# Expert slots through a table in memory, the residual kept on the chip, logits from uncentred rows

## The chip, the cores and the metric

One core of a Trainium2 chip runs the whole program. The time is device microseconds (us) of one execution. Its engines run side by side, each its own list of instructions in the order in which it was written, and wait for one another on semaphores: TensorE (PE), VectorE (DVE), ScalarE (ACT), GpSimd (POOL) and SyncE (SP). DMAs are issued by SP, ACT and POOL and carried out by 16 DMA engines.

## The reference

A two-layer trunk over 512 tokens of width 1024, all in fp32. Layer 0 mixes with chunked gated linear attention (GLA), layer 1 with forgetting attention (FoX); after each mixer comes a layer norm and a mixture of 16 experts:

```python
h = layer_norm(ALPHA * h + mix, ln_g[layer, 0], ln_b[layer, 0])
ffn = grouped_moe(h, router_w, router_bias, moe_w_gate[layer], moe_w_up[layer], moe_w_down[layer])
h = layer_norm(ALPHA * h + ffn, ln_g[layer, 1], ln_b[layer, 1])

def layer_norm(x, g, b):
    mu = mean(x); var = mean((x - mu) ** 2)
    return (x - mu) * rsqrt(var + 1e-5) * g + b

def grouped_moe(x, router_w, ...):            # x: 512 x 1024
    scores = softmax(x @ router_w)            # 16 experts in 4 groups
    # best group by the sum of its top-2 scores (+ bias), then the top-2 experts inside it
    gates = ...                               # two nonzero weights a token, summing to 1
    h = silu(x @ w_gate[e]) * (x @ w_up[e])   # for each expert e, width 512
    y = sum over e of (gates[:, e] * h) @ w_down[e]
```

## The kernel before

There are T = 4 tiles of 128 rows, K = 8 slices of 128 columns and E = 16 experts. An fp32 product is made as three faster ones, of the high and low parts of both sides (L717, L718, L719). A weight comes from memory into a ring in SBUF, ACT casts it to its high part, DVE subtracts that to get the low part, PE uses both.

**Weights.** SP loads them in the order of use: pieces of 2 MB for the mixers (L458), halves of 1 MB for the experts (L506). A load into a ring slot that was used before waits on `w_free`, which PE raises by a marker, a tiny product (L758) at the end of the last unit that reads the slot. A unit is one row tile by 512 columns, 24 products. Between pieces SP issues small loads: the router weights and the layer norms' `ln_b` (L475, L477) behind the piece n == 3.

**GLA.** The units are followed by the heads. For each head and tile PE makes an output in one of two PSUM banks (L1099, L1104), ACT copies it out (L1513) and squares it (L1517); PE reuses a bank when ACT has copied it.

**Entry of the experts.** The out-projection's units add to the residual `H` (DVE, L1649, L1652). DVE subtracts the mean and multiplies by `ln_g` (L1661), then multiplies by the inverse deviation and adds `ln_b` (L1694). PE turns the centred rows (`turn_centred`, L814), ACT copies them, PE makes the router's logits (L822); DVE scales them, adds the part that comes from `ln_b` (`shift_logits`) and picks two experts a token (`router`, L1734 to L1784). `ranks` says which slot of an expert a token has.

**Experts.** For expert e the slot table is a product of a one-hot matrix, made by DVE (`one_hots4`, L2233), and the tokens' numbers and gates (PE, L870; L878 for the first three); DVE takes it into `tokv` and `tokg` (L1820, L1821), which hold TABLES = 6 experts. POOL gathers the token rows by it (L607), always three experts ahead, PE turns them (L885), multiplies by gate and up, turns the hidden rows (L894), multiplies by down; POOL adds the result into `sum_rows` in memory by an indirect DMA (L613). `sum_rows` begins as the residual, which ACT's queue stores there (L1365, four DMAs of 512 KB a layer) while the first expert's weights are made ready.

**Exit.** When 14 experts are scattered and the check for overfull ("cold") experts is through, SP loads `sum_rows` over `H` (L486). The last two experts' results are added by PE (L850, L858); in layer 1 PE adds the residual too (L844). DVE sums (L1961, L1972), ACT takes the variance (L1449), POOL the inverse deviation (L672, L580), DVE scales (L1986, L2000), and PE turns the rows for the next layer (L711).

All orders are written out by hand, engine by engine; no planner moves them.

## Time and profile before

| | |
|---|---|
| Median of 3 runs | 1231.17 us (1229.59 to 1233.8) |
| Profiled execution | 1230.52 us, of which the span is 1228.8 us |
| PE busy | 1193.8 us, 97% of the span |
| DVE, ACT, POOL busy | 893.2 (73%), 703.7 (57%), 183.9 (15%) us |
| Mean granted TensorE clock | 0.992 |
| DMA | 281.52 MB, mean 229 GB/s |

The span runs from the first to the last recorded instruction; 1.7 us of the execution lie around it. A row of a timeline is: start, duration, engine, line, operation, what it writes and reads, and in brackets the idle time of its engine before it with what ended that. PE's products are pipelined: a record lasts 0.39 us while the next begins 0.23 us later, so what counts is the distance of starts. In the windows the experts' stages (about 262 to 560 and 904 to 1200 us) show the DMA engines busy nearly all the time; the mixers' stages show them mostly idle.

### The profile page before, as it was taken

How to read it: one execution, taken by the hardware profiler on the slowest of the kernel's cores; microseconds unless marked ns; L12 is line 12 of the kernel's file. 1: busy time of each engine (PE TensorE's matmuls, PEld its weight loads, DVE VectorE, ACT ScalarE, POOL GpSimd, SP SyncE). 2: the span in 40 equal slices, each digit the busy share in tenths (PEclk: the TensorE clock that was granted, in tenths of full speed). 3: DMA queues.
4: the chain of work that ended last, by engine and by line, in shares of the span. 5: the costliest groups of instructions: out<-in, count | busy, mean ns of one | idle time of the engine just before them, and what ended most of it. 6: DMA issues, size and time to landing. Idle time of an engine off the chain costs nothing.

```text
span 1228.8 us, 14990 instructions
## 1 busy us (share of the span) xinstructions
PE 1193.8 (97%) x5802; PEld 945.0 (77%) x5803; DVE 893.2 (73%) x1159; ACT 703.7 (57%) x866; POOL 183.9 (15%) x158
## 2 busy tenths in 40 slices
PE   7999999999999999999999999999999999999995
PEld 5787588877888888876887766768878888888873
DVE  5275555678999998989433555675679999998886
ACT  4432523357687786774333554573267778777672
POOL 1000100211132221210000000000212222122111
PEclk9999999999999999999899999999999999999998
DMA  8223021179999999987111420322289999999973
GB/s 286 71 85 122 1 103 70 52 257 411 358 368 378 368 370 377 358 340 281 69 70 52 154 86 18 103 84 88 78 314 381 373 362 376 379 367 371 370 276 137
DMA packets 66346, 281.52 MB, mean 229 GB/s; under 512 B 12854, under 2 KB 13110, under 8 KB 41698
## 3 DMA queue, kind: packets, MB, share of 16 engines
q1 hardware_dynamic: 49248, 247.55, 53.2%
q0 software_dynamic: 12288, 28.42, 8.1%
q10 hardware_dynamic: 4738, 4.57, 1.1%
q8 instruction: 47, 0.77, 0.3%
q14 instruction: 25, 0.20, 0.0%
HBM read 270.99 MB, written 25.20 MB: 241 GB/s over the span
## 4 chain that ended last, share of the span: by engine, by line
PE 83%; DMA 7%; DVE 6%; issue 2%; ACT 1%; POOL 0%; DVEq 0%; SPq 0%; ACTq 0%; POOLq 0%
PE ps L717 22%; PE ps L719 22%; PE ps L718 22%; DMA ring<-in_moe_w_up_dram 4%; PE ps L885 2%; PE ps L1168 2%; PE ps L1178 2%; DVE ring_r L1613 2%; PE ps L1191 2%; DMA ring<-in_moe_w_down_dram 1%; PE ps L894 1%; DMA ring<-in_kv_w_dram 1%; PE ps L822 1%; PE ps L1099 1%; PE ps L1087 1%
## 5 line engine op out<-in xcount | busy, mean ns | idle before, releaser
L1613 DVE TENSOR_TENSOR ring_r<-ring,ring_r 128x2048 fp32r<-128x2048 f32 x128 | 291.7, 2284 | 7.8 <-ACT ring_r L1346 7.8
L1346 ACT CAST ring_r<-ring 128x2048 fp32r<-128x2048 f32 x128 | 242.6, 1927 | 15.7 <-DMA ring<-in_moe_w_gate_dram 9.8
L718 PE MATMUL ps<-ring_r,xgT_r 128*128 128x512 f32 x528 | 205.9, 390 | 0.0
L1346 ACT CAST high_r<-ring 128x2048 fp32r<-128x2048 f32 x64 | 122.2, 1913 | 113.4 <-DMA ring<-in_moe_w_up_dram 113.4
L1613 DVE TENSOR_TENSOR ring_r<-ring,high_r 128x2048 fp32r<-128x2048 f32 x64 | 146.1, 2289 | 36.3 <-ACT high_r L1346 35.9
L613 POOL DMA_INDIRECT sum_rows<-arena,tokv x28 | 57.7, 2062 | 389.6 <-ACT arena L1399 389.6
L718 PEld LDWEIGHTS ps<-ring_r,xgT_r 128*128 128x128 f32 x528 | 99.3, 188 | 18.8
L717 PE MATMUL ps<-ring_r,xgT_r 128*128 128x512 f32 x272 | 109.1, 401 | 0.2 <-DVE ring_r L1613 0.2
L719 PE MATMUL ps<-ring_r,xgT_r 128*128 128x512 f32 x272 | 106.1, 390 | 0.0
L717 PE MATMUL ps<-high_r,xgT_r 128*128 128x512 f32 x256 | 102.9, 402 | 1.2 <-DVE xgT_r L1827 1.1
L717 PE MATMUL ps<-featT,ring_r 128*128 128x512 f32 x256 | 103.8, 405 | 0.0
L717 PE MATMUL ps<-ring_r,featT 128*128 128x512 f32 x256 | 102.4, 400 | 0.0
L1607 DVE TENSOR_TENSOR ring_r<-ring,ring_r 128x1024 fp32r<-128x1024 f32 x72 | 84.4, 1221 | 23.3 <-ACT ring_r L1259 23.3
L718 PE MATMUL ps<-ring_r,featT 128*128 128x512 f32 x256 | 100.3, 392 | 0.0
L719 PE MATMUL ps<-ring_r 128*128 128x512 f32 x256 | 100.3, 392 | 0.0
L719 PE MATMUL ps<-high_r,xgT_r 128*128 128x512 f32 x256 | 100.1, 391 | 0.0
L719 PE MATMUL ps<-featT,ring_r 128*128 128x512 f32 x256 | 100.1, 391 | 0.0
L718 PE MATMUL ps<-ring_r 128*128 128x512 f32 x256 | 99.8, 390 | 0.0
L717 PE MATMUL ps<-ring_r,hidT_r 128*128 128x512 f32 x240 | 93.8, 391 | 1.0 <-DVE ring_r L1613 1.0
L719 PE MATMUL ps<-ring_r,hidT_r 128*128 128x512 f32 x240 | 93.5, 390 | 0.0
L718 PE MATMUL ps<-ring_r,hidT_r 128*128 128x512 f32 x240 | 93.4, 389 | 0.0
L607 POOL DMA_INDIRECT arena<-h_rows,tokv x32 | 70.6, 2205 | 69.9 <-DVE tokg L1821 37.9
(288 smaller groups left out, 2118.8 us busy)
## 6 DMA issues: line engine op xcount, KB each, us to landing
ring<-in_moe_w_gate_dram SPq DMA_DIRECT2D x64, 1024.0 KB, 12.2
ring<-in_moe_w_up_dram SPq DMA_DIRECT2D x64, 1024.0 KB, 13.0
ring<-in_moe_w_down_dram SPq DMA_DIRECT2D x64, 1024.0 KB, 12.4
ring<-in_gla_w_in_dram SPq DMA_DIRECT2D x6, 2048.0 KB, 9.8
ring<-in_kv_w_dram SPq DMA_DIRECT2D x4, 2048.0 KB, 12.8
ring<-in_fox_w_qg_dram SPq DMA_DIRECT2D x4, 2048.0 KB, 8.1
ring<-in_gla_w_out_dram SPq DMA_DIRECT2D x2, 2048.0 KB, 7.8
h_rows<-arena POOLq DMA_DIRECT2D x8, 512.0 KB, 2.9
```

The lines of the kernel that those rows point to most:

```text
L607: pool.indirect_dma_start(out=dst, out_offset=None, in_=h_rows, in_offset=bass.IndirectOffsetOnAxis(ap=rows, axis=0), bounds_check=last_ro ...
L613: pool.indirect_dma_start(out=sum_rows, out_offset=bass.IndirectOffsetOnAxis(ap=rows, axis=0), in_=src, in_offset=None, bounds_check=last_ ...
L717: pe.matmul(o, left[0], right[0], start=k == 0, stop=False)
L718: pe.matmul(o, left[0], right[1], start=False, stop=False)
L719: return pe.matmul(o, left[1], right[0], start=False, stop=k == n_k - 1)
L885: mm = pe.transpose(ps[:, kk, j * P:(j + 1) * P], src[:, (4 * kk + j) * P:(4 * kk + j + 1) * P], ident[:, :])
L1168: pe.matmul(ps[:, SCORE + a, 0:(i + 1) * P], kq[rows, p % 3, 1, i * P:(i + 1) * P], kq[rows, p % 3, 0, 0:(i + 1) * P], start=True, stop=Tr ...
L1178: mm = pe.transpose(ps[:, TURNED + a, n * P:(n + 1) * P], prob[:, s % 3, a, n * P:(n + 1) * P], ident[:, :])
L1191: mm = pe.matmul(ps[a * DH:(a + 1) * DH, VALUE, n * P:S], v_b[:, n, c:c + DH], prob_t[:, a, n, n * P:S], start=n == 0, stop=n == T - 1, sk ...
L1346: act.copy(high, w).then_inc(half_high, 1)
L1607: dve.tensor_tensor(low, w, high.bitcast(F32), ALU.subtract).then_inc(w_low, 1)
L1613: dve.tensor_tensor(low, w, high.bitcast(F32), ALU.subtract).then_inc(half_low, 1)
```

## The change

Three edits come together.

1. **Slots.** Only the first three experts' tables are made by PE and DVE (TABLES = 3). For the other thirteen, DVE works out for each token its two places in a table (`find_picks`, ten small operations); POOL writes them with eight indirect DMAs into a table in memory, waits for them, loads the table into SBUF (`slot_tab`), waits for it, and only then issues the gather for expert 3. The tables in memory are first filled with empty slots during GLA.
2. **Residual.** `H` keeps the residual. `sum_rows`, now one per layer, begins as zeros, which ACT's queue stores during GLA in two DMAs. At the exit the sums are loaded beside `H`, and POOL adds them in four operations of 128x1024.
3. **Logits.** PE turns the rows before they are centred, half by half between half units of the out-projection; the router's weights are multiplied by `ln_g` beforehand, and DVE subtracts the mean times the weights' column sums. For that `ln_g` is loaded by SP in two small DMAs, turned by PE, and multiplied in by DVE during GLA. The last tile's scaling is split into two halves placed between the router's first operations.

```diff
-    TABLES = 6
+    TABLES = 3
@@ SP: straight
                     load(mix_piece(n)[2], src)
...
+                    if n == 5:
+                        for L in range(DEPTH):
+                            sp.dma_start(gain_rows[L * K:(L + 1) * K, :], ln_g[L, 0:1, :].rearrange("a (k p) -> (a k) p", p=P)
+                                         ).then_inc(shift_loaded, 16)
@@ SP: load_sums
+                sp.wait_ge(half_used, half_count(L, half_of("up", E - 1, 1)))
                 for t in range(T):
-                    sp.dma_start(H[:, t, :], sum_rows[t * P:(t + 1) * P, :]).then_inc(sums_loaded[t], 16)
+                    sp.dma_start(moe_sums[:, t, :], sum_rows[L][t * P:(t + 1) * P, :]).then_inc(sums_loaded[t], 16)
@@ POOL
+            def store_picks(L):
+                pool.wait_ge(picks_known, L + 1)
+                pool.wait_ge(tables_stored, 16 * (DEPTH + 2 * T * L))
+                for t in range(T):
+                    for j in range(2):
+                        pool.sem_inc(moves, 1)
+                        pool.indirect_dma_start(out=slot_tables[L],
+                                                out_offset=bass.IndirectOffsetOnAxis(ap=pick_at[:, t, j:j + 1], axis=0),
+                                                in_=pick_row[:, t, j, :], in_offset=None, bounds_check=last_slot,
+                                                oob_is_err=False).then_inc(tables_stored, 16)
+                pool.wait_ge(tables_stored, 16 * (DEPTH + 2 * T * (L + 1)))
+                pool.dma_start(slot_tab[:, :, :], slot_tables[L][E:, :].rearrange("(p e) c -> p e c", e=E)
+                               ).then_inc(slots_loaded, 16)
+                pool.wait_ge(slots_loaded, 16 * (L + 1))
...
                 for e in range(3):
...
+                store_picks(L)
                 for e in range(E + 1):
...
                 pool.sem_inc(cold_end, 1)
+                pool.wait_ge(h_ready, T * (2 * L + 1))
+                for t in range(T):
+                    pool.wait_ge(sums_loaded[t], 16 * (L + 1))
+                    pool.tensor_tensor(H[:, t, :], H[:, t, :], moe_sums[:, t, :], ALU.add).then_inc(h_ready, 1)
@@ PE: out-projection
+            def out_unit(L, u0, m):
+                unit(u0 + m, ks=range(K // 2))
+                if m:
+                    turn_rows_half(L, u0, m - 1)
+                unit(u0 + m, frees=2 if m == 2 * T - 1 else 0, ks=range(K // 2, K))
+                for n in LOGITS_AFTER[L].get(m, ()):
+                    logits_half(L, u0, n)
@@ PE: experts
-                    if e + 3 < E:
-                        pe.wait_ge(hot, E * L + e + 4)
-                        pe.wait_ge(tbl_ev, 2 * (E * L + e + 3))
-                        table(e + 3, onehot[:, (e + 3) % 2, :]).then_inc(tbl_done, 1)
@@ PE: GLA
             for u in range(2 * H_A, U_GLA_TAIL):
+                if u == U_GLA_TAIL - 4:
+                    pe.wait_ge(shift_loaded, 16 * (2 * DEPTH + 1))
+                    pe.wait_ge(z_min, T)
+                    pe.wait_ge(z_abs, T)
+                    pe.transpose(ps[:, 6, P:P + DEPTH * K], gain_rows, ident[0:DEPTH * K, 0:DEPTH * K]
+                                 ).then_inc(shift_done, 1)
@@ ACT: experts
-                for t in range(T):
-                    act.wait_ge(h_scaled, T * L + t + 1)
-                    act.dma_start(sum_rows[t * P:(t + 1) * P, :], H[:, t, :]).then_inc(sums_begun, 16)
@@ ACT: GLA
             take(U_GLA_TAIL - 3)
             take(U_GLA_TAIL - 1)
+            act.wait_ge(consts, 20)
+            for L in range(DEPTH):
+                act.dma_start(sum_rows[L].rearrange("(p r) (c n) -> p (r c) n", p=P, n=P),
+                              zeros.unsqueeze(1).to_broadcast([P, T * K, P])).then_inc(sums_clear, 16)
@@ DVE: rows_normed and router
+                        dve.wait_ge(rows_turned, turned_halves(L, t))
...
+                do(dve.tensor_tensor(rt[9], over_e(ln_mv[:, :, 0]), each_t(shift_logits[:, DEPTH + L, :], E), ALU.mult))
+                dve.wait_ge(rows_centred, T * L + T)
+                scale_last(2 * L, 0)
                 dve.wait_ge(rt_logits, L + 1)
...
                 dve.tensor_tensor(rt[0], logits, over_e(rv[0]), ALU.subtract).then_inc(rt_in, 1)
+                scale_last(2 * L, 1)
                 dve.wait_ge(rt_exp, L + 1)
@@ DVE: experts
+                find_picks(L)
+                take_rows(0)
                 low_half(L, 2)
-                take_rows(0)
...
-                    if e + 3 < E:
-                        dve.wait_ge(tbl_done, E * L + e + 2)
-                        one_hots4(dve, onehot_of(e + 3), hot, ranks, slot1, e + 3)
```

The two small `ln_g` loads stand on SP behind the GLA piece n == 5, the sixth. `gain_rows` lies in the arena. SP's list before:

```order
L458 DMA ring<-in_gla_w_in_dram 128x8x512 [waits w_free]
L475 DMA arena<-in_router_w_dram 128x128
L477 DMA arena<-in_ln_b_dram 128x8 x2
L458 DMA ring<-in_gla_w_in_dram 128x8x512 [waits w_free] x2
L458 DMA ring<-in_gla_w_out_dram 128x8x512 [waits w_free] x2
```

And of the change:

```order
L476 DMA ring<-in_gla_w_in_dram 128x8x512 [waits w_free]
L493 DMA arena<-in_router_w_dram 128x128
L495 DMA arena<-in_ln_b_dram 128x8 x2
L476 DMA ring<-in_gla_w_in_dram 128x8x512 [waits w_free] x2
L499 DMA arena<-in_ln_g_dram 8x128 x2
L476 DMA ring<-in_gla_w_out_dram 128x8x512 [waits w_free] x2
```

The two loads went in behind the sixth piece, which itself waits for `w_free`. PE's list of the change, where unit 11 of GLA ends with its marker (L811, before it L758) and unit 12 begins:

```order
L771 MATMUL ps<-ring_r,featT 128x512
L772 MATMUL ps<-ring_r 128x512
L811 MATMUL ps<-ident 128x2
L1165 MATMUL ps<-ident,arena 128x16 [waits z_abs,z_min,shift_loaded]
L770 MATMUL ps<-ring_r,featT 128x512 [waits w_low,ev_dve]
L771 MATMUL ps<-ring_r,featT 128x512
```

L1165, the turning of `gain_rows`, is new and stands directly behind the marker. ACT's list of the change at the end of the GLA units, where L1330 takes unit outputs and L1569 the heads' (before L1277 and L1513):

```order
L1330 COPY arena<-ps 128x512 [waits proj_done] x2
L1563 DMA sum_rows<-arena 4096x1x128 [waits consts]
L1563 DMA sum_rows<-arena 4096x1x128
L1569 COPY arena<-ps 128x256 [waits o_done,act_step]
L1573 ACTIVATE arena<-arena 128x256 [waits o_ev]
```

The two L1563 are new; each is 4096 rows of 512 bytes. POOL's list at the start of the experts, before:

```order
L607 DMA arena<-h_rows,tokv 128x1024 [waits tbl_ev]
L607 DMA arena<-h_rows,tokv 128x1024 [waits tbl_ev,xt_done] x2
L613 DMA sum_rows<-arena,tokv 512x1024 [waits y_ev,sums_begun]
L607 DMA arena<-h_rows,tokv 128x1024 [waits tbl_ev,xt_done]
L613 DMA sum_rows<-arena,tokv 512x1024 [waits y_ev,scattered0]
```

And of the change:

```order
L634 DMA arena<-h_rows,tokv 128x1024 [waits tbl_ev]
L634 DMA arena<-h_rows,tokv 128x1024 [waits tbl_ev,xt_done]
L650 DMA slot_table<-pick_row,pick_at 2064x2 [waits picks_known,tables_stored]
L650 DMA slot_table<-pick_row,pick_at 2064x2 x7
L655 DMA slot_tab<-slot_table 128x32 [waits tables_stored]
L634 DMA arena<-h_rows,slot_tab 128x1024 [waits slots_loaded,xt_done]
L640 DMA sum_rows<-arena,tokv 512x1024 [waits y_ev,sums_clear]
```

Nine DMAs and two waits came between the third and the fourth gather.

## Rows read from the trace of the kernel before

**Rows 1.** The page, part 4: the chain that ended last, by engine.

```profile
PE 83%; DMA 7%; DVE 6%; issue 2%; ACT 1%; POOL 0%; DVEq 0%; SPq 0%; ACTq 0%; POOLq 0%
```

**Rows 2.** PE's timeline (start, us, instruction, idle before) in GLA.

```profile
88.90 0.28 PE L758 MATMUL ps<-ident 128*128 128x2 f32 x2
...
100.87 0.41 PE L1114 MATMUL ps<-arena,one 128*128 128x32 f32 x2 [0.68 <-DVE arena L2091]
```

**Rows 3.** SP's DMAs by line: ns of an issue, first and last start, us to landing.

```profile
L458 SPq DMA_DIRECT2D ring<-in_gla_w_in_dram x3: 367/378/378, 42.7 to 89.2; - x3
L458 SPq DMA_DIRECT2D ring<-in_gla_w_out_dram x1: 367/367/367, 113.8 to 113.8; - x1
...
DMA to landing us min/median/max: 7.6/7.8/7.9
...
L477 SPq DMA_DIRECT2D arena<-in_ln_b_dram x2: 432/514/597, 43.8 to 44.2; - x2
...
DMA to landing us min/median/max: 6.9/7.0/7.1
...
L458 SPq DMA_DIRECT2D ring<-in_gla_w_in_dram x3: 443/1638/5622, 2.9 to 5.1; - x3
```

**Rows 4.** Windows behind a gap of PE: busy of each engine, then clock, DMA share, GB/s.

```profile
611.00:614.00 3.00, 3.00 (x8) 2.41 (x9) 0.64 (x3) 2.06 (x4) 0.00 (x0) 0.50 0.02 5
614.00:617.00 3.00, 3.00 (x14) 2.42 (x13) 0.96 (x2) 2.99 (x4) 0.00 (x0) 0.95 0.00 0
```

**Rows 5.** First heads of GLA on ACT and PE; queue 10 (ACT's); a full window.

```profile
117.61 0.37 ACT L1513 COPY arena<-ps 128x256 f32<-128x256 f32 x1 [3.32 <-PE ps L1104]
...
121.01 0.70 PE L1099 MATMUL ps<-arena 128*128 128x256 f32 x2
...
q10 hardware_dynamic: 4738, 4.57, 1.1%
...
280.00:286.00 6.00, 4.72 (x26) 3.72 (x25) 4.00 (x3) 4.01 (x3) 0.00 (x0) 1.00 1.02 427
```

**Rows 6.** DVE's timeline at the entry of layer 0's experts.

```profile
251.64 2.21 DVE L1694 SCALAR_TENSOR_TENSOR arena<-resid,ln_r,arena 128x1024 f32<-128x1024 f32 x1 [0.54 <-POOL ln_r L580]
254.48 0.22 DVE L1734 TENSOR_TENSOR arena<-ps,ln_r 128x64 f32<-128x64 f32 x1 [0.64 <-PE ps L822]
```

**Rows 7.** Layer 0's experts: PE, the chain's DMA, POOL's gathers, one landing.

```profile
356.21 0.59 PE L870 MATMUL ps<-featT 128*128 128x4 f32 x4
356.66 0.48 PE L717 MATMUL ps<-ring_r,xgT_r 128*128 128x512 f32 x1
...
471.40 16.48 DMA ring<-in_moe_w_up_dram
...
269.06 0.99 POOL L607 DMA_INDIRECT arena<-h_rows,tokv  x1 [3.93 <-PE ps L885]
289.08 2.24 POOL L607 DMA_INDIRECT arena<-h_rows,tokv  x1 [19.04 <-DVE tokg L1821]
...
DMA to landing us min/median/max: 9.7/9.7/9.7
...
307.75 1.03 PE L885 MATMUL ps<-ident,arena 128*128 128x128 f32 x8
```

**Rows 8.** Exits, layer 0 then layer 1, and POOL's operation on 128x128.

```profile
L486 SPq DMA_DIRECT2D resid<-sum_rows x4: 331/432/434, 557.9 to 559.3; - x4
...
DMA to landing us min/median/max: 6.2/7.5/8.7
...
572.01 0.19 POOL L672 TENSOR_SCALAR ln_r<-ln_mv 128x1 f32<-128x1 f32 x1 [21.85 <-ACT arena L1449]
...
DMA to landing us min/median/max: 3.1/4.9/6.6
...
1210.98 0.19 POOL L672 TENSOR_SCALAR ln_r<-ln_mv 128x1 f32<-128x1 f32 x1 [21.72 <-ACT arena L1449]
...
3.17 0.29 POOL L555 TENSOR_SCALAR_AFFINE_SELECT ident<-ident 128x128 f32<-128x128 f32 x1 [0.16 <-POOL row_id L552]
```

248 lines of the change are left out of this document (147 added, 101 removed).

## The prediction, made before the changed kernel ran

> **What bounds the kernel now.** I read the page first. PE is busy 97% of the span at a mean clock of 0.992, and the chain that ended last is PE for 83% of its length, DMA for 7%, DVE for 6% [rows 1]. So two kinds of place decide: where PE runs on without a gap, whatever makes it wait is paid in full; and in the experts' stages, where the chain holds single weight loads 16.48 us long [rows 7] and the window shows the DMA engines full at 427 GB/s [rows 5], bytes count as much as PE's work. Then I read PE's timeline around each place where the changed order gives it a new wait, SP's issues and landings there, and ACT's and POOL's timelines where new DMAs stand in their lists.
>
> **GLA, the turned gains: +7.8.** PE's marker of unit 11 starts at 88.90 [rows 2]. It alone releases the load of the sixth piece, which SP issues at 89.2 and which lands 7.8 later, at 97.0 [rows 3]. The new `ln_g` loads stand behind that load on SP, and PE's new transpose, which waits for them, stands directly behind that marker. Do small loads pass a large one? The `ln_b` loads were put behind the piece issued at 42.7, which landed after 7.9 at 50.6; issued at 43.8 and 44.2, they took 6.9 and 7.1 and landed at 50.7 and 51.3 [rows 3], so they didn't. The gains land at about 97.4, PE goes on at 97.7 instead of 89.15: +8.5. The wait of 0.68 at 100.87 for DVE's sums [rows 2] goes, since DVE has time to catch up: +7.8. Queued behind the transpose is all that PE has left in GLA; DVE's new five operations (two multiplications, a reduction) need the transposed gains too, but DVE's result is read two units, some 11 us, later. The price from below: if the small loads did pass, their issue and a bare landing of some 2.5 us, so +1.8. Nothing gives this back, as PE has no gap up to the experts.
>
> **The clock behind gaps: +2.0.** Behind a gap of PE the granted clock was 0.50 (the lower level, 1.2 GHz) for the window 611 to 614, with 8 products in it, against 14 in the next 3 us at 0.95 [rows 4]: six products fewer at 0.21 us (3 us over 14), 1.3 us lost. An idle stretch of 8.5 us should cost one such loss, the next term's half of one. From 0 to 2.6.
>
> **GLA, the zeros: +6.8.** ACT has 3.32 us of idle before it copies the first head's output at 117.61 [rows 5], so it is free from 114.3. There it now issues two DMAs of 4096 rows of 512 bytes. Do issues hold the engine? SP's first three piece loads, 1024 rows each, took 443, 1638 and 5622 ns to issue [rows 3]: with 3072 rows under way the third was held. So I take it that ACT is held until all but some 3000 of the 8192 rows are gone, 63% of the transfer. The transfer of 4.2 MB takes 9.8 us at 427 GB/s [rows 5] from below, and from above 45.6 ns a packet (queue 10: 1.1% of 16 engines' 1228.8 us over 4738 packets, rows 5), 23.4 us; I take 13, nearer to the row that shows bulk. 63% is 8.2. The out-projection's 2 MB, released by the last GLA marker, is under way at the same time (113.8, landing in 7.6 [rows 3]), and takes 4.9 us of the engines. ACT is free at 114.3 + 13.1 = 127.4. PE needs the first head's bank again for its third output at 121.01 [rows 5], so ACT would have had to be there by 120.5: PE waits 6.9, call it 6.8. Bounds: 0 if the issues hold nobody, 13 by the dearer packets.
>
> **Entries of the experts: −1.1 for both.** In layer 0 DVE scales the last tile (2.21) from 251.64, then waits 0.64 for PE's logits [rows 6]; the logits now don't wait for centring, and that wait goes. Half of the scaling lies in the wait for ACT's exponentials, about 0.3 saved; one more router operation costs 0.25 (start to start of its small operations), the split 0.1. That is −0.55 a layer; from −1.5 to +1 a layer, the latter if the turned halves come late and DVE's centring, which now waits for them, is late with them.
>
> **Experts: −1.5 a layer, −3.0.** Off PE go 13 tables at 0.45 (356.21 to 356.66, rows 7): 5.9. Off the DMA engines go 2.1 MB of stored residual at 427 GB/s [rows 5]: 4.9. As both bound the stage, the smaller counts, and not all of it: the loads early in the stage are held by ring slots, not by bytes, so I keep 3.7; the tiny writes cost 0.5 of it. The rest is the fourth gather. POOL is free at 270.05 and the next gather was issued at 289.08 [rows 7]. Now there stand eight indirect DMAs before it. The price of one issue is 0.99 (at 269.06) to 2.24 (at 289.08) [rows 7], with 0.3 between; at that time DVE works on weights, as at 289, so 2.24: 270.05 + 8 x 2.54 = 290.4. Then the last write lands and the table is loaded, each at a price the trace doesn't show in this place; between 2.6 and 9.7 (the gather's landing), I take 4.5 each: 299.4. The gather lands 9.7 later plus its issue beyond the first bytes, about 310. PE turned those rows at 307.75 [rows 7], 1.35 earlier now without three tables: it waits 3.5 (0 by the cheap issue, 15 by the long landings). The loads run on meanwhile until the ring is full, so I charge half, 1.7: −3.7 + 0.5 + 1.7 = −1.5. From −5 to +6 a layer.
>
> **Exits: +3.0 and +0.5.** In layer 0 SP's loads of the sums, issued 557.9 to 559.3, land from 564.1 to 568.0 [rows 8]. POOL now adds tile by tile before its first inverse deviation, which stood at 572.01. No such operation is in the trace; one input over 128x128 took 0.29 [rows 8], eight of these 2.3; twice that, 4.6, for two inputs from above. I take 2.7: 564.1 + 4 x 2.7 = 574.9, +2.9, and 0.1 for SP's added wait. By 2.3 it is +1.3, by 4.6 +10. Queued behind it are DVE's scaling and PE's transposes for the next layer. In layer 1 the loads are issued at 1197.4 and the first lands after 3.1 [rows 8]: 1200.5 + 10.8 = 1211.3 against 1210.98, +0.5 with the wait of PE's residual product; from 0 to 7.
> Beside the sum, which doesn't need it: the Trainium skill, "GPSIMD Engine Reference", section 3.1, gives 4497 ns for an fp32 `tensor_tensor` of 2048 elements; half, an estimate of 2.25 us for 1024, would make the first exit +1.1. But the Trainium skill, "SBUF — State Buffer", section "SBUF: two separate sides", has a GpSimd operation that reads SBUF and a DVE operation with two SBUF inputs shut each other out for their whole length. No run here shows it yet; it is the mechanism of the last rival.
>
> **Sum.** 7.8 + 2.0 + 6.8 − 1.1 − 3.0 + 3.0 + 0.5 = +16.0 on the profiled execution of 1230.52: 1246.5. The median of before is 0.65 above that execution, so 1247.2. The three new constants cost under 0.2 at the start and are left out.
>
> **Rivals.**
> - *The zero stores hold nobody* (chance 0.25). ACT goes on at once, and 6.8 and half a clock loss (0.7) go: +8.5, 1239.7. For it: a later 2 MB load's issue took 378 ns [rows 3]. Against it: that was one load into an empty queue; the third of three was held for 5.6.
> - *The experts give all that is taken off* (0.18). This is the side of "not slower". Its place is the two long stages: −4.9 each, the gather on time by issues of 0.99 [rows 7], the adds hidden, ACT held by nothing: 7.8 + 1.3 − 1.1 − 9.8 + 0.5 + 1.0 = −0.3, 1230.9. It decides from the point where a fourth gather's issue is before about 296. For it: a chain that holds 16.48 us loads [rows 7]. Against: eight issues and two landings in a row. If also the small loads pass the piece, another −6, 1225.
> - *POOL is shut out* (0.15). Where DVE works with two inputs, the four adds cost 4.6 each and the eight issues more, as far as 15 us late: +7 at the first exit, +3 at the second, +2 a layer at the gather: 16.0 + 14 = +30 at most, with half of it +23, 1254.
> - The forecast itself has 0.42.
>
> A measurement of this kernel can tell from no change about 0.3%, 3.7 us: 1227.5 to 1234.9. Faster than that is part of the second rival, 0.06; within it the rest of that rival and a little of the first, 0.14; slower 0.80. The likeliest case has its own range, 1241 to 1254; for 8 in 10 the range takes in the first rival, half of the last and the upper edge of the second: 1233 to 1258.
>
> **What would show it.** PE's row behind unit 11's marker in GLA with a wait of 8 us on a DMA of `ln_g`, and no wait at the shift product; its absence would take away half of the forecast. ACT's two zero DMAs with an issue of 5 us or more, and PE's third head output late. In the experts: POOL's eight indirect DMAs and their length, the fourth gather near 300, PE's transposes for expert 3 with a wait of 3 to 4; shorter landings of the weight loads. At the exit: four POOL additions of 2.3 to 3 us and the first inverse deviation some 3 us later. The prediction is wrong if the GLA stretch up to 248 isn't 10 us longer or more, or if a stage of experts is more than 4 us shorter.

## The result, and the profile after

The changed kernel takes 1275.18 us in the median of 4 runs (1270.57 to 1279.92) against 1232.49 for the kernel before in the same comparison: a ratio of 1.034, 95% interval 1.0286 to 1.0395. It is slower, as forecast, but by 42.7 us and not 16; the time lies outside the range of 1233 to 1258. The profiled execution took 1275.37 us, its span 1273.7, 44.9 more than before.

The page of the changed kernel: part 1, and part 4, which answers to [rows 1].

```profile
PE 1205.2 (95%) x5699; PEld 949.9 (75%) x5700; DVE 891.7 (70%) x1106; ACT 704.3 (55%) x866; POOL 229.0 (18%) x189
...
PE 77%; DMA 11%; DVE 6%; issue 2%; ACT 1%; ACTq 1%; POOL 1%; DVEq 0%; SPq 0%; POOLq 0%
```

PE is busy 11.4 us longer, although the 104 small products of 26 tables were taken off it, and the mean granted clock fell from 0.992 to 0.969. So the 44.9 us are of two kinds: about 33 of new idle time on PE, and products that ran at the lower level of the clock. In the chain, DMA's share rose from 7% to 11%, and ACT's queue and POOL, both 0% before, now hold 1% each.

What PE waited for in the changed kernel, the longest groups (after the colon: us in all, times, longest), without two that the kernel before has at nearly the same size:

```profile
PE ps L1165 <- DMA arena<-in_ln_g_dram: 8.3, 1, 8.3
PE ps L764 <- DVE resid L2086: 5.9, 1, 5.9
PE ps L1150 <- ACT arena L1569: 5.7, 1, 5.7
PE ps L941 <- DMA arena<-h_rows,slot_tab: 5.0, 1, 5.0
...
PE ps L890 <- DVE picked_b L1843: 4.1, 2, 2.1
PE ps L907 <- DVE y_lo L1984: 3.9, 1, 3.9
```

The forecast had the first and the third (8.5, 6.8), something like the fourth (3.5), and 3 us in the place of the second. The last two it did not have.

To say where the time lies I cut both profiled executions at the same instructions of PE and took the stretches between them (us):

| Stretch | before | after | more | forecast |
|---|---|---|---|---|
| start to the marker of GLA's unit 11 | 88.9 | 89.4 | 0.5 | 0 |
| to the marker of unit 15 (turned gains) | 24.6 | 34.8 | 10.2 | 7.8 + 1.3 |
| GLA's heads, to the next marker (zeros) | 57.3 | 64.7 | 7.4 | 6.8 + 0.7 |
| layer 0's out-projection, to its last marker | 77.1 | 79.8 | 2.7 | 0 |
| entry, to the first product of an expert | 22.0 | 26.1 | 4.1 | −0.55 |
| layer 0's experts, to the first product with `y_hi` | 294.5 | 297.4 | 2.9 | −1.5 |
| exit of layer 0, to FoX's first marker | 37.7 | 45.2 | 7.5 | 3.0 |
| FoX, to the last marker of its out-projection | 285.1 | 287.9 | 2.8 | 0 |
| entry of layer 1 | 22.4 | 26.6 | 4.2 | −0.55 |
| layer 1's experts | 294.4 | 295.6 | 1.2 | −1.5 |
| PE's sums at the end, and the rest | 24.8 | 26.1 | 1.3 | 0.5 |

Stretches on which a kernel changes nothing agree within 0.5 us in most executions; FoX alone runs from 285.0 to 288.3, by the length of its first units. Its out-projection can be told from that: from its next to last marker to its last it took 52.6 us in every kernel without the logits part and 55.4 with it (53.5 in e5, below), so the 2.8 are the change's. A clock that falls in one execution and not in another can move an entry by some 5 us and an experts' stage by 2. What is read below from less than that rests on more than one kernel, or is called open.

**The gains.** PE's timeline after, behind the marker of unit 11 (before: [rows 2]):

```profile
97.95 0.28 PE L1165 MATMUL ps<-ident,arena 16*128 16x16 f32 x1 [8.25 <-DMA arena<-in_ln_g_dram]
```

The small loads did not pass the sixth piece. Behind this wait the clock was low; the window after it:

```profile
98.00:104.00 6.00, 6.00 (x16) 4.73 (x17) 4.25 (x10) 0.00 (x0) 0.00 (x0) 0.54 0.00 0
```

Its columns are those of [rows 4]. 16 products in 6 us at 0.54, where 14 went into 3 us at 0.95 in [rows 4]: about 12 fewer, 2.6 us, where the forecast had put 1.3.

**The zeros.** ACT and ACT's queue at the end of GLA's units, then PE (before: [rows 5]):

```profile
124.42 12.51 ACTq L1563 DMA_DIRECT2D sum_rows<-arena  x2
...
137.02 0.37 ACT L1569 COPY arena<-ps 128x256 f32<-128x256 f32 x1 [12.02 <-issue]
...
137.44 1.22 PE L1150 MATMUL ps<-arena 128*128 128x256 f32 x2 [5.66 <-ACT arena L1569]
```

The two issues hold ACT for 12.5 us (forecast: 13.1), and PE waits 5.66 (forecast: 6.8).

**The entry.** DVE and PE of layer 0 after, and the window behind:

```profile
272.87 4.82 PE L854 MATMUL ps<-high_r 128*128 128x512 f32 x20
...
279.48 0.20 DVE L1843 CAST picked_b<-arena 128x64 bf16<-128x64 f32 x1
...
279.73 0.18 PE L890 MATMUL ps<-picked_b,upto_b 128*128 128x16 bf16 x1 [2.04 <-DVE picked_b L1843]
...
282.00:296.00 14.00, 14.00 (x52) 12.00 (x52) 7.03 (x24) 5.52 (x6) 3.75 (x4) 0.55 0.86 319
```

The same phase before, as far behind the picks (which came at 258.95), ran at the full clock:

```profile
262.00:276.00 14.00, 12.57 (x72) 10.26 (x71) 11.44 (x16) 6.45 (x5) 3.13 (x3) 1.00 0.81 269
```

L854 is the filler that keeps PE at work while DVE picks the experts. The picks come 10.84 us after the last marker instead of 11.09: 0.25 earlier, so far as I had worked out. But PE's logits are ready 2.2 us earlier (the filler behind them starts 4.23 us after the last marker, not 6.44), and the filler is still 20 products long; they are through 2 us before the picks. PE idles 2.04 us, and 52 products instead of 72 go into these 14 us, at 0.55.

**Layer 0's experts.** POOL, DVE and PE around the fourth gather, after (before: [rows 7]):

```profile
295.38 2.37 POOL L650 DMA_INDIRECT slot_table<-pick_row,pick_at  x1 [0.30 <-issue]
...
315.56 0.60 POOL L655 DMA_DIRECT2D slot_tab<-slot_table  x1 [4.47 <-DMA slot_table<-pick_row,pick_at]
...
321.80 2.30 DVE L1669 TENSOR_TENSOR ring_r<-ring,ring_r 128x2048 fp32r<-128x2048 f32 x1
321.87 7.55 POOL L634 DMA_INDIRECT arena<-h_rows,slot_tab  x1 [5.71 <-DMA slot_tab<-slot_table]
324.00 4.50 DVE L1669 TENSOR_TENSOR ring_r<-ring,high_r 128x2048 fp32r<-128x2048 f32 x2
...
336.88 1.97 PE L941 MATMUL ps<-ident,arena 128*128 128x128 f32 x8 [4.97 <-DMA arena<-h_rows,slot_tab]
```

The writes' issues took 0.98 to 2.60 us, 1.70 in the mean, less than the 2.24 assumed: from POOL being free to the gather's issue 26.8 us went by, for 29.4 forecast. The gather's own issue, from 321.87, lasts 7.55 us, while DVE works with two inputs, and the rows landed 15.0 us after its start; layer 1's took 1.05 at 979.00. PE turned the rows of layer 0 at 336.88, against 307.75 before.

**The exits.** POOL, DVE and PE at layer 0's, after (before: [rows 8]):

```profile
591.88 4.56 DVE L1663 TENSOR_TENSOR ring_r<-ring,ring_r 128x1024 fp32r<-128x1024 f32 x2 [0.18 <-ACT ring_r L1312]
592.21 13.03 POOL L718 TENSOR_TENSOR resid<-resid,arena 128x1024 f32<-128x1024 f32 x4 [14.13 <-DMA arena<-sum_rows]
596.97 6.06 DVE L1663 TENSOR_TENSOR ring_r<-ring,ring_r 128x1024 fp32r<-128x1024 f32 x2
...
608.47 1.97 PE L764 MATMUL ps<-ident,resid 128*128 128x128 f32 x8 [5.87 <-DVE resid L2086]
```

And at layer 1's:

```profile
1240.37 5.90 DVE L1977 TENSOR_SCALAR featT<-slot,arena 128x128 fp32r<-128x128 f32 x8
1241.39 9.44 POOL L718 TENSOR_TENSOR resid<-resid,arena 128x1024 f32<-128x1024 f32 x4 [11.87 <-DMA arena<-sum_rows]
...
1247.61 0.77 PE L907 MATMUL ps<-y_hi,featT 128*128 128x512 f32 x1 [3.88 <-DVE y_lo L1984]
```

An addition took 3.26 us beside DVE's pairs (13.03 over 4) and 2.36 in layer 1 (9.44 over 4). What I had left out is the other side: DVE's pairs took 4.56 and 6.06 us, where the same pairs took 2.36 and 2.35 before, and its eight `TENSOR_SCALAR`s 5.90 instead of 1.66.

### The profile page after: what moved, and what is told of

It reads as the page before. It is cut to its first block, busy times and chain, and to the rows that moved or that the text cites. A ratio compares the mean times of both kernels' runs of the same rounds, so it can differ in the third digit from the quotient of the medians.

```text
span 1273.7 us, 14726 instructions
## 1 busy us (share of the span) xinstructions
PE 1205.2 (95%) x5699; PEld 949.9 (75%) x5700; DVE 891.7 (70%) x1106; ACT 704.3 (55%) x866; POOL 229.0 (18%) x189
## 4 chain that ended last, share of the span: by engine, by line
PE 77%; DMA 11%; DVE 6%; issue 2%; ACT 1%; ACTq 1%; POOL 1%; DVEq 0%; SPq 0%; POOLq 0%
PE ps L770 20%; PE ps L772 20%; PE ps L771 20%; DMA ring<-in_moe_w_up_dram 5%; DVE ring_r L1669 2%; PE ps L1225 2%; PE ps L1235 2%; PE ps L941 2%; PE ps L1248 1%; DMA ring<-in_moe_w_down_dram 1%; PE ps L854 1%; DMA arena<-h_rows,slot_tab 1%; PE ps L764 1%; ACTq L1563 1%; PE ps L879 1%
## 5 line engine op out<-in xcount | busy, mean ns | idle before, releaser
L1669 DVE TENSOR_TENSOR ring_r<-ring,ring_r 128x2048 fp32r<-128x2048 f32 x128 | 289.9, 2286 | 13.3 <-ACT ring_r L1401 13.1
L1663 DVE TENSOR_TENSOR ring_r<-ring,ring_r 128x1024 fp32r<-128x1024 f32 x72 | 90.3, 1303 | 22.8 <-ACT ring_r L1312 22.7
L770 PE MATMUL ps<-ring_r,featT 128*128 128x512 f32 x256 | 104.7, 409 | 0.0
L771 PE MATMUL ps<-ring_r,featT 128*128 128x512 f32 x256 | 101.3, 396 | 0.0
L640 POOL DMA_INDIRECT sum_rows<-arena,slot_tab x22 | 45.1, 2049 | 310.7 <-ACT arena L1451 269.2
L1312 ACT CAST ring_r<-ring 128x1024 fp32r<-128x1024 f32 x72 | 71.0, 1045 | 12.8 <-PE ps L811 6.0
```

Source lines behind the costliest of these rows:

```text
L640: pool.indirect_dma_start(out=sum_rows[L], out_offset=bass.IndirectOffsetOnAxis(ap=rows, axis=0), in_=src, in_offset=None, bounds_check=la ...
L770: pe.matmul(o, left[0], right[0], start=k == 0, stop=False)
L771: pe.matmul(o, left[0], right[1], start=False, stop=False)
L1312: act.copy(high, w).then_inc(w_high, 1)
L1663: dve.tensor_tensor(low, w, high.bitcast(F32), ALU.subtract).then_inc(w_low, 1)
L1669: dve.tensor_tensor(low, w, high.bitcast(F32), ALU.subtract).then_inc(half_low, 1)
```

## The experiments

Theory and rivals came to this. **Theory:** the 44.9 us are the sum of local stalls that the table names, each to be removed by a local edit. **Rivals:** the experts' stages or the clock give back what a local edit saves; the many small DMAs slow the weight loads; the filler's gap is chance. The first four kernels ran twice each, and the intervals of their ratios overlap that of the changed kernel; what an edit gave is therefore read from its own stretches.

### Four edits of the changed kernel

The gains' loads earlier on SP (e1):

```diff
-                    if n == 5:
+                    if n == 3:
                         for L in range(DEPTH):
                             sp.dma_start(gain_rows[L * K:(L + 1) * K, :], ...
```

> The changed kernel with one edit: the two small ln_g loads stand behind the fourth piece (n == 3) on SP, beside the ln_b loads, instead of behind the sixth (n == 5). Theory (the turned gains wait for a load that is queued behind a piece which PE's own marker releases): PE's wait of 8.25 us before the transpose goes, with it the stretch at half clock behind it; the marker of unit 15 comes at 114.0 instead of 124.2, the whole is 10 us shorter, about 1265. Rival (small loads are slow by themselves, wherever they stand): the wait stays over 4 us.

Measured: 1264.12 us, ratio to before 1.0272 (1.0222 to 1.0322), 11 under the changed kernel. PE's turning of the gains by line (ns, first to last start):

```profile
L1165 PE MATMUL ps<-ident,arena x1: 232/232/232, 88.6 to 88.6; 16*128 16x16 f32 x1
```

It waits for nothing, and the stretch to unit 15's marker is 25.6 instead of 34.8: −9.2. The wait and the clock behind it are shown.

The zeros issued by SP behind the seventh piece, and not by ACT (e2):

```diff
+                    if n == 6:
+                        sp.wait_ge(consts, 20)
+                        for L in range(DEPTH):
+                            sp.dma_start(sum_rows[L]..., zeros...).then_inc(sums_clear, 16)
-            for L in range(DEPTH):
-                act.dma_start(sum_rows[L]..., zeros...).then_inc(sums_clear, 16)
```

> The changed kernel with one edit: the two stores of zeros are issued by SP behind the seventh piece instead of by ACT before the first head. Theory (the issue holds the engine that makes it, until most rows are gone): ACT's 12 us hold and PE's wait of 5.66 at the third head output go, the heads stage is 7.4 us shorter, total about 1268; SP shows the long issue instead. Rival (the transfers themselves disturb the heads or the loads, whoever issues them): heads as long as now, or the cast of the out-projection's weights late by some us.

Measured: 1267.23, ratio 1.0297 (1.0231 to 1.0363), 8 under. SP's queue, and ACT's first copy of a head:

```profile
123.48 11.87 SPq L500 DMA_DIRECT2D sum_rows<-arena  x2
...
126.84 0.37 ACT L1570 COPY arena<-ps 128x256 f32<-128x256 f32 x1 [3.32 <-PE ps L1160]
```

Now SP is held, for 11.9 us, and nobody needs it; ACT's idle time is the 3.32 us of [rows 5] again, and the heads take 57.3 us, as before: −7.4. (The two experts' stages of this execution differ from the changed kernel's by −4.8 and +3.7; that isn't this edit's doing, and is taken up below.)

More filler at the entries, 28 products for 20 (e3):

```diff
-                idle_products(20, 4)
+                idle_products(28, 4)
```

> The changed kernel with one edit: PE's row of filler products at the router has 28 instead of 20. Theory A (the logits come 1.4 us earlier, the filler now ends 2 us before the picks are known, the clock falls to its lower level for the tables and the turning that follow): no gap of PE over 0.3 us before the ranks, clock 1.0 through the entry, the entry 3.5 us shorter in each layer, total 1268. Theory B (the clock falls for another reason, such as the small shapes of the logits): the clock still falls, and the entry is as long or 0.3 longer.

Measured: 1276.17, ratio 1.037 (1.0299 to 1.0441): nothing gained, a miss. PE at layer 0's entry, and the window of the same place as above:

```profile
279.35 0.18 PE L890 MATMUL ps<-picked_b,upto_b 128*128 128x16 bf16 x1 [0.26 <-DVE picked_b L1843]
...
288.60 1.97 PE L941 MATMUL ps<-ident,arena 128*128 128x128 f32 x8 [2.07 <-DMA arena<-h_rows,tokv]
...
282.00:296.00 14.00, 11.93 (x55) 9.75 (x55) 9.25 (x24) 6.67 (x6) 6.19 (x5) 0.76 0.84 323
```

The gap before the ranks is gone (2.04 to 0.26), and the entries are 2.2 and 3.6 us shorter. But part of the gap only moved: PE, now earlier, waits 2.07 us for the first gathered rows (2.06 in layer 1), and the clock falls behind that, so that the 14 us are at 0.76, up from 0.55, and not at 1.00. Layer 0's experts gain 0.7 us (the fourth gather is late again, PE waits 3.21). Layer 1's take back 4.4, since PE waits 8.0 for `y_lo` instead of 3.9. So the local half of the theory holds in part, and so does the rival of "given back".

The residual added by DVE, tile by tile just ahead of its sums, and not by POOL (e4):

```diff
-                for t in range(T):
-                    pool.wait_ge(sums_loaded[t], 16 * (L + 1))
-                    pool.tensor_tensor(H[:, t, :], H[:, t, :], moe_sums[:, t, :], ALU.add).then_inc(h_ready, 1)
+                def add_moe(t):
+                    dve.wait_ge(sums_loaded[t], 16 * (L + 1))
+                    dve.tensor_tensor(H[:, t, :], H[:, t, :], moe_sums[:, t, :], ALU.add).then_inc(h_ready, 1)
```

> The changed kernel with one edit: DVE, not POOL, adds the loaded sums to the residual, tile by tile. Theory (POOL's additions and DVE's work on the weights shut each other out: 3.26 us an addition, DVE's pairs of low parts 4.56 and 6.06 instead of 2.36): DVE's low parts take 1.2 each again, the PE wait of 5.87 before the first turned rows shrinks to below 2, the first exit is 5 us shorter; in the second, DVE's eight one-hot operations take 1.65 instead of 5.90, PE's wait of 3.88 goes, but DVE's four additions (1.3 each) partly take its place: 0 to 4 shorter. Total about 1268. Rival (the exit is long because the loads of the sums come late): the exits stay within 1 us.

Measured: 1263.18, ratio 1.0264 (1.0177 to 1.0351), 12 under. DVE's and PE's timeline at layer 0's exit:

```profile
586.02 2.36 DVE L1659 TENSOR_TENSOR ring_r<-ring,ring_r 128x1024 fp32r<-128x1024 f32 x2
591.17 1.22 DVE L2040 TENSOR_TENSOR resid<-resid,arena 128x1024 f32<-128x1024 f32 x1
...
597.65 1.56 PE L760 MATMUL ps<-ident,resid 128*128 128x128 f32 x8 [1.93 <-DVE resid L2086]
```

With POOL's additions away DVE's pairs are back at 2.36 (from 4.56 and 6.06); DVE does an addition in 1.22 where POOL took 2.4 to 3.3; PE's wait at L764 falls from 5.87 to 1.93, and layer 1's for `y_lo` is gone. The exit takes 41.6 instead of 45.2. The mutual hold-up of DVE and POOL is shown. Not all of the 12 us is this edit's: layer 0's experts are 5.5 shorter, where it touches nothing, and layer 1's entry 2.9, by the clock. The exit's 3.6 is its part, and so is what it takes off layer 1's experts, 4.6 at most (more on this below). By the Trainium skill, "SBUF — State Buffer", section "SBUF: two separate sides", the pair of ports that the two share is locked for whole instructions; the trace agrees in the mechanism that both lose: 3.26 for 2.36 on POOL, 4.56 and 6.06 for 2.36 on DVE.

**What differs by chance of timing.** Two waits come and go between kernels whose edit has nothing to do with them. The first is the fourth gather of layer 0. Its issue took 7.55, 6.96, 7.48 and 7.44 us in the changed kernel, e1, e3 and the kernel with all four edits (f), and 1.04 in e2 and e4. DVE and POOL in e1, then in e4:

```profile
311.53 2.30 DVE L1669 TENSOR_TENSOR ring_r<-ring,ring_r 128x2048 fp32r<-128x2048 f32 x1
312.19 6.96 POOL L634 DMA_INDIRECT arena<-h_rows,slot_tab  x1 [5.73 <-DMA slot_tab<-slot_table]
```

```profile
320.92 1.04 POOL L634 DMA_INDIRECT arena<-h_rows,slot_tab  x1 [5.69 <-DMA slot_tab<-slot_table]
321.42 2.29 DVE L1665 TENSOR_TENSOR ring_r<-ring,ring_r 128x2048 fp32r<-128x2048 f32 x1
```

The long ones began 0.07 to 0.66 us after DVE had begun an unbroken row of three subtractions with two inputs from SBUF, and ended 0.92 us after that row. The short ones began while DVE read PSUM, 0.32 and 0.50 us before the row. The twenty such gathers of the ten kernels with the slot table fit one pattern: begun beside an operation with two inputs from SBUF the issue ends 0.92 to 1.02 us after the end of these operations, begun beside one that reads PSUM it takes 1.04 or 1.05. That is an order in time in twenty places, and not an edit of that alone. The stage goes with it: layer 0's experts took 297.4, 298.5, 296.7 and 297.7 us with the long issue, 292.6 and 291.9 with the short, where PE did not wait (in e4 the rows landed 5.9 us after the issue's start).

The second is layer 1's `y_lo`. Its wait follows how much of DVE's eight `TENSOR_SCALAR`s falls beside POOL's additions. In e1 they were over 0.24 us before the first addition (1.65 us, no wait, stage 291.1); in the changed kernel they began 1.02 before it (5.90, wait 3.88, stage 295.6); in e2, 0.30 before it (10.09, wait 7.91, stage 299.3).

### The three parts alone

Each is the kernel before with one part of the change; the fourth kernel is the whole change with all four edits above. The profiled execution of the slots part is the slowest of its four, 1244.06 against a median of 1239.22, so its stretches are some 5 us too long in all.

> The first part alone on the kernel before: slots of thirteen experts by the table in memory, residual and logits as before. Theory (the late fourth gather and its clock loss cost 5 to 7 in layer 0 and little in layer 1; the 5.9 us of PE taken off come back only in part, since the stored residual still fills the DMA engines): 1231 to 1238. Rival (the table is a gain of its own, PE's 5.9 a layer): 1222 to 1226.

> The second part alone: residual kept in SBUF, sums from zeros. Theory: the zeros' issue +7.4 in GLA, the exits +7.5 and +4.9, the experts 2 to 3 shorter a layer for the missing 2.1 MB: +12 to +16, 1244 to 1247. Rival (the stored residual was in nobody's way, no gain in the experts): 1251.

> The third part alone: logits from uncentred rows. Theory: the gains' load +10.2, the out-projections +2.7 each (logits moved ahead of the last unit), the entries +3 to +4 each by the clock behind a filler that ends too early: +22 to +24, 1254. Rival (the clock in the entries falls by the slot table's work, not by the logits): entries not longer than before, total 1246 to 1248.

> The changed kernel with the four edits of before together: ln_g loads behind the fourth piece, zeros issued by SP, 28 filler products, additions on DVE. Theory (the four add up, apart from what the experts' stage takes back of the entry): 1275 less 10, 7.4, 7 and 0 to 5: 1247 to 1251. Rival (the places hide one another, or the gaps come back elsewhere through the clock): over 1255.

| Kernel | us | ratio to before (95%) | more than before |
|---|---|---|---|
| slots alone (p1) | 1239.22 | 1.0049 (1.0032 to 1.0065) | 6 |
| residual alone (p2) | 1255.04 | 1.0185 (1.0168 to 1.0202) | 22 |
| logits alone (p3) | 1252.66 | 1.0158 (1.0138 to 1.0179) | 19 |
| all, with the four edits (f) | 1247.55 | 1.0115 (1.0093 to 1.0137) | 14 |

The parts add up to 47, together they cost 43: nearly a sum, so they hardly meet. No part is a gain. The slots came out 1 us above the expected range, the residual part 8. Its stretches: +8.5 at the heads (zeros), +7.1 at the exit, +6.3 in layer 1's experts, whose end is PE's wait:

```profile
1225.29 0.77 PE L857 MATMUL ps<-y_hi,featT 128*128 128x512 f32 x1 [8.15 <-DVE y_lo L1906]
```

It is 8.15 us, and not 3.9: POOL's first addition came 0.32 us after the start of the `TENSOR_SCALAR`s, as in e2. The logits alone have the wait for the gains (8.20), the out-projection's +2.7 and the entry's gap (2.05); their entries are 4.2 and 1.3 longer, and layer 0's experts give 2.0 of it back. The four edits together take off 27.6 us; what they leave is the out-projections, an exit of 41.6 against 37.7, entries of 23.9 and 24.4, and the late gather of layer 0 (PE waits 5.68).

### What holds the weight loads in the slots part?

The eight writes alone, into a table that nobody reads, in the kernel before (x1):

```diff
+                for m in range(2 * T):
+                    pool.indirect_dma_start(out=spare_tables[L], ..., in_=spots[:, 2 * T:2 * T + 2], ...
```

> The kernel before, with eight more indirect DMAs a layer, issued by POOL behind the third gather: each writes 128 rows of 8 bytes, 128 bytes apart, into a spare table in memory that nobody reads. This is what the slot table's writes do, without any wait for them. Theory A (the small writes cost the DMA engines work that their bytes don't show: in the first 20 us of the experts the share is 1.0 but the rate 304 to 335 GB/s instead of 370 to 422, some 1.4 MB less, and the first part alone made the experts' stages 4.7 longer): the rate falls in the same way, the stages get 3 to 4 us longer, total 1239 to 1241. Theory B (the stage is longer by the late fourth gather and POOL's waits, the writes cost nothing): total 1232 to 1234.

Measured: 1231.13, ratio 0.999 (0.9972 to 1.0007): the writes cost nothing, the rival of slowed loads falls. Their issues ranged from 0.98 to 2.54 us, and the engines moved what they moved before (402 and 395 GB/s). The first 20 us of layer 0's experts, in the kernel with the writes:

```profile
271.20:291.20 20.00, 18.71 (x90) 15.39 (x91) 16.18 (x13) 12.12 (x10) 12.14 (x10) 1.00 1.02 402
```

The same in the slots part alone, where DVE also works out the places:

```profile
271.30:291.30 20.00, 18.72 (x83) 15.22 (x83) 16.53 (x11) 10.39 (x9) 12.22 (x9) 0.93 1.02 328
```

At the same share of busy time (1.02) 328 GB/s went through and not 402. Neither the clock nor the order of DVE's steps explains it, since x4, with that order undone, ran here at the full clock and 338 GB/s. One difference is that these writes go where the picks say and x1's to rows 128 bytes apart; no run tells whether that matters.

The second half of the question: PE's work of the 13 tables is gone, why is the stage not shorter? I gave PE the work back as products that nobody needs (x3):

```diff
+                    if e + 3 < E:
+                        for _ in range(6):
+                            pe.matmul(ps[:, 7, 0:4], ident[:, :], ident[:, 0:4], start=True, stop=True)
```

> The first part alone, with six tiny products of PE (0.45 us) put where each of the thirteen later tables was made. Theory (the loads bound the stage; PE's shorter experts only reach their limit earlier): experts at a pace of 18.15 instead of 17.7 us, the loads follow for longer, and each stage is as long as in the first part alone, within 1.5: total 1238 to 1241. Rival (PE's work is what counts): +5.9 a layer, 1249 to 1251.

Measured: 1247.59, ratio 1.0131 (1.0111 to 1.0151): outside the theory's range, and nearer to the rival's. But the edit isn't the test that it was meant to be. The products cost 1.35 us an expert and not 0.45: PE took 19.05, where it took 18.2 before. The starts of two successive turns (kernel before, then this one, then the slots part):

```profile
416.71 1.03 PE L885 MATMUL ps<-ident,arena 128*128 128x128 f32 x8
434.90 1.03 PE L885 MATMUL ps<-ident,arena 128*128 128x128 f32 x8
```

```profile
425.66 1.03 PE L916 MATMUL ps<-ident,arena 128*128 128x128 f32 x8
444.71 1.03 PE L916 MATMUL ps<-ident,arena 128*128 128x128 f32 x8
```

```profile
419.09 1.03 PE L916 MATMUL ps<-ident,arena 128*128 128x128 f32 x8
437.81 1.03 PE L916 MATMUL ps<-ident,arena 128*128 128x128 f32 x8
```

In the slots part an expert of layer 0 takes 17.7 to 18.0 us up to the seventh, but for one of 20.3, and then 18.3 to 19.1 and once 19.9: I read this as the ring running empty, with the loads setting the pace, at about 18.8. Before, PE's own 18.2 held to the eleventh. So a PE that is 0.45 faster reaches the limit of the loads some three or four experts earlier. In x3 PE is slower than that limit and keeps its 19.05 until the last two. Its 17 us more of PE's work a stage (13 times 1.35) made the stages 2.2 and 4.1 us longer than those of the profiled slots part; by the medians, which that execution exceeds by 5, both together cost 8 us of 35, by the ratios 10. So PE's work was free in large part, and not wholly. That the tables as they were, 5.9 us a stage, lay wholly beside the loads, this run can't show; the two kernels of the next section bear on it.

DVE's `low_half(L, 2)` ahead of the search for the places, as before the change, with the slots part (x4):

```diff
+                low_half(L, 2)
                 find_picks(L)
                 take_rows(0)
-                low_half(L, 2)
```

> The first part alone, with DVE's low part of the third half done before the picks are found and the first rows taken, as the kernel before has it, instead of behind them. Theory (DVE's order is of no account, the stage suffers from the fourth gather and the clock): stage lengths within 1 of the first part alone, or 1 to 3 longer, since the picks and all that hangs on them come 2.3 later. Rival (the later low part holds the ring and so the loads): the experts' stages get 2 to 4 shorter, total 1232 to 1235.

Measured: 1240.3, ratio 1.0065 (1.0042 to 1.0088), the slots part's time within the intervals. The stages are 2.7 and 5.1 us shorter, as the rival said, but the entries 4.3 and 1.3 longer, and each profile is one execution from the upper end of its kernel's range. So the rival isn't refuted for the stages by themselves; in time the order of these steps gives nothing.

### Bytes instead of products

The residual part, with the zeros from SP and the sums added by the DMA itself, so that neither POOL nor DVE adds (b1; b2 is the same with the slots part too):

```diff
-                    pool.tensor_tensor(H[:, t, :], H[:, t, :], moe_sums[:, t, :], ALU.add).then_inc(h_ready, 1)
+                    pool.indirect_dma_start(out=H[:, t, :], out_offset=None, in_=sum_rows[L],
+                                            in_offset=bass.IndirectOffsetOnAxis(ap=spots[:, t:t + 1], axis=0),
+                                            ..., compute_op=ALU.add).then_inc(sums_loaded[t], 16)
```

> The second part alone, with the zeros issued by SP, and the scattered sums added to the residual in SBUF by four indirect DMAs of POOL that add as they land, in place of SP's loads and POOL's additions. Theory: heads as before (0 instead of +8.5), experts 1.5 to 1.8 shorter a layer for the missing store, exits as before plus the slower landing of POOL's DMAs: total 1226 to 1232, perhaps faster than before. Rival (the adding DMAs land 5 us or more later than SP's loads, and the exit of layer 0 waits): 1235 to 1240.

> First and second part together, without the third, zeros issued by SP, the sums added into SBUF by POOL's adding DMAs. Theory (both bounds move at once: 2.1 MB less for the DMA engines, 5.9 us less for PE): experts 2 to 3.5 shorter a layer than in the kernel before where the fourth gather is on time, entries 1.4 longer, total 1226 to 1232. Rival (the late fourth gather and its clock take it all): 1234 to 1238.

Measured: 1232.9 for the first, ratio 0.9999 (0.9984 to 1.0014), and 1237.82 for the second, which has the slots part too, ratio 1.0058 (1.0039 to 1.0077). Both missed their expected 1226 to 1232; the second lies in its rival's range. The first takes all 22 us off the residual part: heads 57.3, exit 37.9, experts 292.6 and 292.4. The experts are 1.9 and 2.0 us shorter than before, and in the residual part's layer 0, behind an entry as before, 1.5: so 2 MB of stores less in a stage give some 1.5 to 2.0, where their bytes alone come to 4.9. The profiled execution has this back at layer 0's entry, 5.2 longer by a lower clock, and in FoX, 1.6 longer; that the median of twelve executions has nothing left of the 3.9 isn't explained. With the slots as well the experts take 292.5 and 291.9, hardly less: the tables taken off PE gave 0.1 and 0.5. That is read from the fastest execution of that kernel, 1233.46; its median lies 5 us above the first's.

### The entry and the out-projection

Twelve filler products for twenty in the kernel before (x2):

```diff
-                idle_products(20, 4)
+                idle_products(12, 4)
```

> The kernel before, with 12 instead of 20 filler products of PE at the router, so that PE stands still for 1.8 us before the picks are known. Theory (this gap is what drops the clock in the entries of the changed kernel): clock 0.50 for 7 to 14 us from there, the entry of the experts 3.5 to 4 us longer in each layer, less what DVE and POOL hide: total 1237 to 1241. Rival (a gap of 2 us does nothing to the clock): as before.

Measured: 1234.96, ratio 1.0015 (0.9994 to 1.0036). PE and the windows behind the picks, in layer 0 and in layer 1:

```profile
259.12 0.18 PE L833 MATMUL ps<-picked_b,upto_b 128*128 128x16 bf16 x1 [1.90 <-DVE picked_b L1770]
...
262.00:276.00 14.00, 13.52 (x52) 11.62 (x53) 7.08 (x15) 4.92 (x5) 3.13 (x3) 0.61 0.75 277
...
900.00:914.00 14.00, 11.74 (x71) 9.35 (x72) 10.19 (x26) 8.92 (x10) 3.14 (x3) 0.88 0.75 262
```

The time is below the theory's range. A gap of 1.90 brought the low clock in layer 0 (entry 26.9 instead of 22.0); one of 1.89 in layer 1 did not (22.5 against 22.4, and the kernel before shows the same 0.88 in this window without a gap). In all profiles the layer 0 entry was 26.1 to 26.9 in the six kernels with a gap of 1.9 to 2.1 us there. Nine of the other eleven took 21.9 to 24.0, but b1 took 27.2 and x4 27.7: there the clock fell at 251, with no gap before it but one of 0.2. In layer 1, of six kernels with such a gap, three took 26.2 to 26.6 and three 22.5 to 23.7. So a gap of 2 us goes with a fall of the clock often and not always, a fall needs no such gap, and over ten executions the gap cost 1.9 us, with zero still inside the interval.

The logits part with the gains early, the logits of three half tiles behind the last marker, where the kernel before has them, and 24 filler products (e5):

```diff
-        LOGITS_AFTER = ({m: (m - 1,) for m in range(1, 2 * T)}, {1: (0,), 3: (2, 1), 4: (3,), 5: (4,), 6: (5,), 7: (6,)})
+        LOGITS_AFTER = ({m: (m - 1,) for m in range(1, 2 * T - 3)}, {1: (0,), 3: (2, 1), 4: (3,)})
...
-                    if n == 5:
+                    if n == 3:
...
-                idle_products(4, 7)
+                for n in (4, 5):
+                    logits_half(L, OUT_UNITS[L], n)
-                idle_products(2, 7)
+                logits_half(L, OUT_UNITS[L], 6)
-                idle_products(20, 4)
+                idle_products(24, 4)
```

> The third part alone, with the ln_g loads behind the fourth piece, 24 filler products, and the logits of the last but one tile behind the last unit's marker, where the kernel before has them, instead of between the last units. Theory (work that PE did while DVE was on the last tile was moved ahead of the last unit, where nothing hides it: 2.7 a layer): the stretch up to the last marker is 1.8 to 2 shorter than in the third part alone, the entry behind it no longer; with the stall and the clock mended, total 1234 to 1238. Rival (the 2.7 are the switching between units and half turns): the stretch shortens by under 0.5, total 1239 or more.

Measured: 1237.15, ratio 1.003 (1.0011 to 1.0048), where the logits part alone has 1.0158. The out-projection is down from 79.8 to 77.9 (77.1 before): the products that the change put ahead of the last marker cost there, and behind it PE did them while it had only DVE to wait for. The filler is now too long instead: DVE waits 2.32 us for PE's ranks, where it waited 0.29 before, and the entries are 1.5 and 0.8 longer than before.

## Why the prediction was wrong in size

- **The gains, 7.8, and the clock behind them, 1.3: right.** 10.2 for 9.1, shown by e1's −9.2.
- **The zeros, 6.8 + 0.7: right.** 7.4, shown by e2. That the issue holds its engine for most of the transfer was the disputed step; it held it for 12.5 us.
- **The out-projections, nothing: wrong, by 5.5.** I had taken it that PE's turns and logits only change places. But before they stood behind the last marker, in PE's idle time, where filler covers the wait for DVE; moved ahead of it they are on the path, 2.7 and 2.8, and what they freed behind it is empty. The failed step is "PE's order costs nothing if its products are the same"; e5 shows it with −1.9.
- **The entries, −1.1: the step that failed most by the table, +8.3.** The working of DVE's side was good to 0.3 us. The failed step is the filler: I never asked what PE does when its logits are ready 2 us earlier and the picks are not. It runs out of filler, 2.04 us, and the clock falls. My term for "the clock behind gaps" counted only the gaps of GLA. Of six kernels with such a gap the clock fell in layer 0 in all, and in layer 1 wholly in three; it also fell twice without one, e3 took 5.8 of the 8.3 away and gained no time, and x2 made such a gap for 1.9 us. So the 8.3 are where the time of this execution lay, and not what mending it is worth.
- **The experts, −3.0: wrong, +4.1, by the gather's price and by the exit, and not by the credit.** Up to the fourth gather's issue layer 0 was quicker than worked out, 26.8 us for 29.4: the writes' issues were priced too high, 2.24 for 1.70, and the last landing and the table's load a little too low. What failed is the gather itself, taken at 9.7 us to landing as in [rows 7]: its issue lasted 7.55 and its rows landed after 15.0. PE waited 4.97 and behind it ran at 0.65 for 8 us. That the 3.5 forecast for the wait came near is luck, since without the long issue there was none. In layer 1 the gather was on time; there the stage ends with PE's 3.88 for `y_lo`, which is the exit's doing. Where neither came in, the stages were 1.9 and 2.6 us shorter than before in layer 0 (e2, e4) and 3.3, 3.4 and 2.6 in layer 1 (e1, e4, f), against the 3.2 (3.7 less 0.5) of the forecast. The bytes make 1.5 to 2.0 of that; how much of the rest is PE's tables isn't shown, 0.1 and 0.5 by b2.
- **The exits, 3.5: right in kind, too small in size, 8.8 and the 3.88 just named.** POOL's addition took 3.26 and 2.36 for my 2.7. What failed is that I priced POOL's operations and not those of DVE beside them: the low parts of the next weights took twice as long, and PE's next operands hang on these. e4 shows it with −3.6 at the exit. In layer 1 the wait is gone with it, but e1 lacks the wait too, with POOL's additions, since there they began just after DVE's operations; what shows the cause in layer 1 is that the wait grew with the overlap, 0, 3.88 and 7.9.

Of the rivals the third named the mechanism that was right, POOL and DVE shutting each other out, and saw one side of it; its highest sum, +30, lay 13 us below the result. That the zero stores hold nobody is refuted, and so is that the experts give all that is taken off. What stays open: why the slots part moves 328 GB/s and not 402 in its first 20 us; why the clock falls at an entry in one execution and not in another; and why the gather's issue, once begun beside DVE's two-input operations, lasts to the end of their row. That it does is read from twenty places, but no run varied it alone.

## What to carry to other kernels

Work that stands in the shadow of another engine is free only there: before products are moved ahead, read what they covered, and give the filler behind them a new length. Where the loads set the pace near the end of a stage, a faster engine mainly empties the ring earlier; fewer bytes shorten the stage, here by less than half of their transfer time. An operation given to an idle engine is priced by what it does to the engine with which it shares a port, not by its own length; here the DMA's own addition was the only one that cost nothing. And when one edit removes a wait elsewhere that it doesn't touch, look for an order in time that turned by a few tenths of a us before giving the edit the credit: here such an order moved a stage by 5 us.
